# Experts' rows turned by block transpositions on VectorE, and layer 1's experts with two pieces at least, in a two-layer diffusion backbone with a mixture of experts

## The reference

```python
def _grouped_moe(t, router_w, router_b, w_gate, w_up, w_down):
    ...
    gates = jnp.sum(jax.nn.one_hot(e_idx, N_EXPERTS, dtype=jnp.float32) * w[..., None], axis=1)
    y = jnp.zeros(t.shape, jnp.float32)
    for e in range(N_EXPERTS):
        he = jax.nn.silu(t @ w_gate[e]) * (t @ w_up[e])
        y = y + gates[:, e:e + 1] * (he @ w_down[e]).astype(jnp.float32)
    return y.astype(t.dtype)
```

## Time and profile before

| | us |
|---|---|
| median of 3 runs | 1245.73 (1242.93 to 1247.1) |
| the profiled execution, its own time | 1249.11 |
| its span | 1247.4 |
| PE busy | 955.2 (77%) |
| DVE busy | 418.5 (34%) |
| ACT busy | 363.0 (29%) |
| POOL busy | 66.2 (5%) |
| moved by DMA | 326.56 MB, mean 262 GB/s |

### The profile page before, as it was taken

How to read it: one execution, slowest core, us unless ns; L and a number is a source line. 1 busy time by engine, 2 the same in 40 slices (tenths; PEclk the granted TensorE clock), 3 DMA queues, 4 the chain that set the end, 5 groups by cost and what they waited for, 6 DMA issues and landing times.

```text
span 1247.4 us, 23521 instructions
## 1 busy us (share of the span) xinstructions
PE 955.2 (77%) x9105; PEld 549.4 (44%) x9106; DVE 418.5 (34%) x1124; ACT 363.0 (29%) x744; POOL 66.2 (5%) x106
## 2 busy tenths in 40 slices
PE   5799989989962887888888836998993755556883
PEld 3244554433442443444444415785573422323542
DVE  1366655663143111111111217568624100100112
ACT  3322355552031122222222215227612111110221
POOL 0000000000002000000000020000001000000001
PEclk9899999998966998999999976999996977887995
DMA  9999398797033298896989957005045799999942
GB/s 327 403 354 320 134 387 315 272 337 270 0 135 143 75 337 298 325 361 248 398 302 398 367 204 272 1 19 202 1 145 201 274 396 395 395 393 396 397 174 105
DMA packets 139502, 326.56 MB, mean 262 GB/s; under 512 B 9456, under 2 KB 18048, under 8 KB 139456
## 3 DMA queue, kind: packets, MB, share of 16 engines
q1 hardware_dynamic: 118064, 294.36, 63.4%
q0 software_dynamic: 7200, 22.81, 5.2%
q10 hardware_dynamic: 14192, 8.76, 2.3%
HBM read 308.99 MB, written 33.69 MB: 275 GB/s over the span
## 4 chain that ended last, share of the span: by engine, by line
PE 40%; DMA 12%; SPq 10%; ACT 8%; issue 7%; DVE 6%; ACTq 5%; POOL 1%; DVEq 1%; POOLq 0%
SPq L280 9%; PE bank L592 7%; PE bank L524 7%; PE bank L572 5%; ACTq L823 4%; DMA h_t<-h_rows 4%; PE bank L424 4%; PE bank L494 3%; DMA y_rows<-work 3%; ACT L817 3%; PE bank L367 3%; PE bank L465 2%; DMA ring<-in_w_up_dram 2%; PE bank L477 2%; PE bank L535 1%
## 5 line engine op out<-in xcount | busy, mean ns | idle before, releaser
L572 PE MATMUL bank<-ring,h_t 128*32 128x256 f32 x4160 | 259.1, 405 | 68.8 <-DMA ring<-in_w_up_dram 58.7
L572 PEld LDWEIGHTS bank<-ring,h_t 128*32 128x32 f32 x4160 | 140.9, 117 | 173.5 <-issue 103.8
L592 PE MATMUL bank<-ring,h_t 128*32 128x256 f32 x2080 | 130.7, 393 | 21.5 <-issue 16.2
L817 ACT ACT_TABLE_LOAD x65 | 83.4, 1283 | 154.8 <-issue 145.1
L424 PE MATMUL bank<-h_t,ring 128*128 128x512 f32 (+1 forms) x320 | 118.1, 524 | 12.3 <-ACT h_t L732 12.3
L1157 DVE TENSOR_TENSOR h_t<-h_t,bank 128x128 f32<-128x128 f32 x65 | 18.7, 288 | 257.3 <-ACT h_t L817 257.3
L1154 DVE COPY h_t<-bank 128x256 f32<-128x256 f32 x65 | 27.6, 425 | 213.1 <-PE bank L572 209.6
L563 PE MATMUL bank<-cst,h_t 128*128 128x128 f32 x134 | 29.8, 304 | 87.5 <-DVE h_t L1147 87.5
L592 PEld LDWEIGHTS bank<-ring,h_t 128*32 128x32 f32 x2080 | 66.5, 112 | 65.9 <-issue 31.6
L424 PEld LDWEIGHTS bank<-h_t,ring 128*128 128x128 f32 x320 | 62.5, 196 | 60.7 <-issue 40.9
L524 PE MATMUL bank<-tokm,ring 128*128 128x512 f32 (+1 forms) x256 | 85.3, 496 | 1.0 <-DVE tokm L1019 1.0
(11 more groups left out here) (148 smaller groups left out, 1028.6 us busy)
## 6 DMA issues: line engine op xcount, KB each, us to landing
ring<-in_w_gate_dram SPq DMA_DIRECT2D x32, 2048.0 KB, 13.6
ring<-in_w_up_dram SPq DMA_DIRECT2D x32, 2048.0 KB, 17.4
ring<-in_w_down_dram SPq DMA_DIRECT2D x32, 2048.0 KB, 16.5
ring<-in_ada_w_dram SPq DMA_DIRECT2D x24, 2048.0 KB, 10.1
ring<-in_w_in_dram SPq DMA_DIRECT2D x8, 1536.0 KB, 17.8
h_t<-h_rows POOLq DMA_DIRECT2D x70, 128.0 KB, 5.2
h_rows<-in_table_dram SPq DMA_DIRECT2D x1, 8704.0 KB, 45.0
y_rows<-in_table_dram SPq DMA_DIRECT2D x1, 8704.0 KB, 64.0
```

Of the source, the lines that this page charges most:

```text
L572: last = mm(bank[1][CHUNK * q:CHUNK * q + CHUNK, 0:256], hc_t[:, k, :], w[q // 2][:, k, 256 * (q % 2):256 * (q % 2) + 256], start=(k == 0) ...
L592: last = mm(bank[4][CHUNK * q:CHUNK * q + CHUNK, 0:256], h, wd[:, k, 256 * q:256 * q + 256], start=(k == 0), stop=(k == KF - 1))
L817: do(act_g, turned_he[:, :, 0:2 * CHUNK], ACT.Silu).then_inc(silu_done[l], 1)
```

## The change

Each piece is turned without PE. POOL's load now puts quarter q of the 32 rows on partitions 32q to 32q+31 (`(q c)` split with q outermost), and ACT's copy L809 writes the token rows in an order in which the transposition of 32x32 blocks by DVE gives `hc_t` at once. Gate and up are computed so that partition group q holds, for each of gate and up, columns 32q to 32q+31 of each of the four blocks of 128 (the moving operand has 8 runs of 32 columns out of two slots); then silu and the product read bank 1 directly (ACT L799, DVE L1168 in the new numbering), and one more transposition of blocks on DVE gives `he_t`. `turn_rows`, `turn_he`, bank 3 and bank 5 of the expert part, and the copies L1140 and L1154 are gone.

The stores of result rows move from ACT (four of 32 KB) to POOL (one of 128 KB), and `yrow` has two halves. POOL's loop is: store of piece g, then load of piece g+4; before, it held loads alone. ACT runs silu of g+1 ahead of the copy of g. `LEAST` is [2, 2], so layer 1 takes `expert_long` too, its 11 experts with one piece get a second piece of padding, and w_down's slot is free a piece later. `h_rows` and `y_rows` grow from 2176 to 2304 rows. At the start POOL stores six small blocks of zeros to raise the two semaphores of the stores.

```diff
-LEAST = [2, 1]
+LEAST = [2, 2]
...
-ROWS = P * -(-CHUNK * (max(MAX_CHUNKS) + 3) // P)
+ROWS = P * -(-CHUNK * (max(MAX_CHUNKS) + 5) // P)
...
-                sp.wait_ge(down_mm[l], done)
+                sp.wait_ge(down_mm[l], done + 1)
                 load_expert(l, e + 3, a, (2,))
...
                 def gate_up(g, a):
-                    w = [ring[:, 3 * a + s, :].rearrange("p (k n) -> p k n", k=KD) for s in range(2)]
+                    w = ring[:, 3 * a:3 * a + 2, :].rearrange("p s (k c m) -> p s k c m", k=KD, c=KF)
                     pe.wait_ge(hc_ready[l], g + 1)
+                    pe.wait_ge(he_ready[l], g + 1)
                     for k in range(KD):
                         for q in range(4):
-                            last = mm(bank[1][CHUNK * q:CHUNK * q + CHUNK, 0:256], hc_t[:, k, :],
-                                      w[q // 2][:, k, 256 * (q % 2):256 * (q % 2) + 256],
+                            o = bank[1][CHUNK * q:CHUNK * q + CHUNK, 0:256]
+                            last = mm(o.rearrange("r (s c i) -> r s c i", s=2, c=KF), hc_t[:, k, :],
+                                      w[:, :, k, :, CHUNK * q:CHUNK * q + CHUNK],
                                       start=(k == 0), stop=(k == KD - 1))
                     last.then_inc(gu_mm[l], 1)
...
                     gate_up(g0, a)
-                    turn_rows(g0 + 1)
                     if prev is not None:
                         down(g0 - 1, prev)
-                    weights_in(a, turns, (2,))
-                    turn_he(g0)
                     with pe.Fori(g0 + 1, g1) as g:
                         gate_up(g, a)
-                        turn_rows(g + 1)
+                        weights_in(a, turns, (2,))
                         down(g - 1, a)
-                        turn_he(g)
...
-                with act.Fori(0, all_chunks(act, l)) as g:
-                    act.wait_ge(he_turned[l], g + 1)
-                    do(act_g, turned_he[:, :, 0:2 * CHUNK], ACT.Silu).then_inc(silu_done[l], 1)
-                    act.wait_ge(down_mm[l], g + 1)
-                    act.wait_ge(rows_stored[l], 64 * g + 64)
-                    do(yrow, bank[4][:, 0:256], ACT.Identity).then_inc(rows_ready[l], 1)
-                    act.wait_ge(rows_ready[l], g + 2)
-                    for q in range(4):
-                        act.dma_start(y_rows[bass.ds(CHUNK * g, CHUNK), 256 * q:256 * q + 256],
-                                      yrow[CHUNK * q:CHUNK * q + CHUNK, :]).then_inc(rows_stored[l], 16)
+                def gated(g):
+                    act.wait_ge(gu_mm[l], g + 1)
+                    do(act_g, bank[1][:, 0:P], ACT.Silu).then_inc(silu_done[l], 1)
+
+                def row_out(g):
+                    act.wait_ge(down_mm[l], g + 2)
+                    act.wait_ge(rows_stored[l][0], (g + 2) // 2 * 16)
+                    act.wait_ge(rows_stored[l][1], (g + 3) // 2 * 16)
+                    nc.scalar.copy(yrow[:, bass.ds(g % 2 * 256, 256)], bank[4][:, 0:256]).then_inc(rows_ready[l], 1)
...
+                    gated(0)
+                    with act.Fori(0, total - 1) as g:
+                        gated(g + 1)
+                        row_out(g)
+                    row_out(total - 1)
...
                 with pool.Fori(0, (total + 1) // 2) as m:
                     for i in range(2):
-                        pool.wait_ge(hc_moved[l], 2 * m + 1 + i)
-                        load_rows(2 * m + 2 + i, i)
+                        pool.wait_ge(rows_ready[l], 2 * m + 2 + i)
+                        pool.dma_start(y_rows[bass.ds(CHUNK * (2 * m + i), CHUNK), :].rearrange("r (q c) -> q r c", q=4),
+                                       yrow[:, 256 * i:256 * i + 256]).then_inc(rows_stored[l][i], 16)
+                        pool.wait_ge(hc_moved[l], 2 * m + 3 + i)
+                        load_rows(2 * m + 4 + i, i)
...
+                def rows_turned(n):
+                    dve.wait_ge(hc_moved[l], n + 1)
+                    v.transpose(hc_t.rearrange("p k r -> p (k r)"), hc).then_inc(hc_ready[l], 1)
...
                     dve.wait_ge(gu_mm[l], g + 1)
-                    v.tensor_copy(he, bank[1][:, 0:256]).then_inc(he_ready[l], 1)
                     rows_turned(g + 1)
                     dve.wait_ge(silu_done[l], g + 1)
-                    v.tensor_tensor(he_t, act_g, turned_he[:, :, 2 * CHUNK:P], ALU.mult).then_inc(het_ready[l], 1)
+                    v.tensor_tensor(he, act_g, bank[1][:, P:2 * P], ALU.mult).then_inc(he_ready[l], 1)
+                    dve.wait_ge(he_ready[l], g + 2)
+                    dve.wait_ge(down_mm[l], g + 1)
+                    v.transpose(he_t.rearrange("p k r -> p (k r)"), he).then_inc(het_ready[l], 1)
                     rows_in(g + 2)
```

More of the change, by code:

```diff
@@ L142, in backbone @@
         h_rows = nc.dram_tensor("h_rows", [ROWS, D], F32, kind="Internal").ap()
-        y_rows = nc.dram_tensor("y_rows", [ROWS, D], F32, kind="Internal").ap()
+        y_rows = nc.dram_tensor("y_rows", [ROWS + CHUNK, D], F32, kind="Internal").ap()
         ident = cst[:, C_ID:C_ID + P]
@@ L174, in backbone @@
         hc_got = hflat[:, 0:512]
-        hc = hflat[:, 1280:1536]
-        hc_t = hflat[:, 512:768].rearrange("p (k r) -> p k r", k=KD)
-        he = hflat[:, 768:1024]
-        act_g = hflat[:, 1024:1152].rearrange("p (j m) -> p j m", j=2)
-        he_t = hflat[:, 1152:1280].rearrange("p (j m) -> p j m", j=2)
+        hc = hflat[:, 512:768]
+        hc_t = hflat[:, 768:1024].rearrange("p (k r) -> p k r", k=KD)
+        act_g = hflat[:, 1024:1152]
+        he = hflat[:, 1152:1280]
+        he_t = hflat[:, 1280:1408].rearrange("p (k r) -> p k r", k=KF)
         pos = work[:, 736:744]
-        yrow = work[:, 0:256]
+        yrow = work[:, 0:512]
         ych = [tokm, hflat.rearrange("p (t n) -> p t n", t=4)]
@@ L210, in backbone @@
         mask_ready, rank_mm, route_ready = sem("mask_ready"), sem("rank_mm"), sem("route_ready")
[L211 removed]
+        rows_zeroed, block_zeroed = sem("rows_zeroed"), sem("block_zeroed")
         hc_in = [[sem(f"hc_in{l}_{i}") for i in range(2)] for l in range(DEPTH)]
[L213 removed]
+        hc_moved, hc_ready = per_layer("hc_moved"), per_layer("hc_ready")
         gu_mm, silu_done, he_ready = per_layer("gu_mm"), per_layer("silu_done"), per_layer("he_ready")
[L215 to L216 removed]
+        het_ready, down_mm, rows_ready = per_layer("het_ready"), per_layer("down_mm"), per_layer("rows_ready")
+        rows_stored = [[sem(f"rows_stored{l}_{i}") for i in range(2)] for l in range(DEPTH)]
         pos_ready, scattered, rows_all = sem("pos_ready"), sem("scattered"), sem("rows_all")
@@ L221, in backbone @@
         dve_step = sem("dve_step")
-        turned_he = bank[3][:, 0:256].rearrange("p (j m) -> p j m", j=2)
         def ada_bank(u):
@@ L589, in down @@
                     for k in range(KF):
-                        h = he_t[:, k % 2, CHUNK * (k // 2):CHUNK * (k // 2) + CHUNK]
                         for q in range(4):
-                            last = mm(bank[4][CHUNK * q:CHUNK * q + CHUNK, 0:256], h,
+                            last = mm(bank[4][CHUNK * q:CHUNK * q + CHUNK, 0:256], he_t[:, k, :],
                                       wd[:, k, 256 * q:256 * q + 256], start=(k == 0), stop=(k == KF - 1))
@@ L630, in experts @@
                 pe.wait_ge(route_ready, l + 1)
-                turn_rows(0)
                 expert(0, 0, 1, None)
@@ L655, in combine @@
                     tile_sums(nt - 1)
+            for l in range(DEPTH):
+                pe.sem_inc(down_mm[l], 1)
             pe.wait_ge(cst_in, 16)
@@ L808, in route @@
                     act.wait_ge(h_turned, 2 * sum(TOK_TILES[:l]) + q + 1)
-                    do(tokm[:, q // 2, 512 * (q % 2):512 * (q % 2) + 512], bank[2 + q % 4][:, :],
+                    rows = tokm[:, q // 2, :].rearrange("p (j k i) -> p k j i", j=4, k=KD)
+                    do(rows[:, 4 * (q % 2):4 * (q % 2) + 4],
+                       bank[2 + q % 4][:, :].rearrange("p (k j i) -> p k j i", k=4, j=4),
                        ACT.Identity).then_inc(tok_ready, 1)
@@ L869, in _ @@
                 norm_shift(2 * l, 512)
+                if l == 0:
+                    for stored in rows_stored:
+                        act.wait_ge(stored[0], 16)
+                        act.wait_ge(stored[1], 32)
                 qkv(l)
@@ L883, in _ @@
         def _(pool):
-            for l in range(DEPTH):
-                pool.sem_inc(rows_stored[l], 64)
+            pool.wait_ge(block_zeroed, 1)
+            for turns in (1, 2):
+                for l in range(DEPTH):
+                    for i in range(turns - 1, 2):
+                        pool.dma_start(y_rows[ROWS:ROWS + CHUNK, :].rearrange("r (q c) -> q r c", q=4),
+                                       ring[:, 8, 0:256]).then_inc(rows_stored[l][i], 16)
+                        pool.wait_ge(rows_stored[l][i], 16 * turns)
             for l in range(DEPTH):
@@ L907, in load_rows @@
```

(8 more changed lines are left out.)

57 lines of the change are left out of this document (26 added, 31 removed).

## The result

| | before | changed |
|---|---|---|
| median, us | 1244.33 (4 runs, 1240.24 to 1247.1) | 1275.13 (4 runs, 1272.29 to 1275.4) |
| ratio, 95% interval | 1 | 1.0245 (1.0211 to 1.0279) |
| span of the profiled execution | 1247.4 | 1273.2 |
| PE / DVE / ACT / POOL busy | 955.2 / 418.5 / 363.0 / 66.2 | 955.6 / 421.8 / 288.8 / 142.9 |

The account below looks back on a forecast made before the run. Bound in layer 0 by a circle of latencies through ACT (7.52 us a piece), in layer 1 by weights at 395 GB/s. -67.5 + 4 - 1.4 = -64.9 us took the 1245.7 us median to 1181 us; range 1164 to 1210.

Parts of the forecast that it names:

- All of it hangs on 395 GB/s: Layer 0's weight stream: 91.8 MB at layer 1's measured 395 GB/s takes 232 us, so the layer ends at 668.
- a longer landing L: Row loads behind a store in POOL's queue: landing taken as 7 us instead of 5.3, bounds 5.3 and 12.
- Layer 0: Layer 0's experts become a stream of weights; last down at 668 instead of 735.5, a gain of 67.5 us.
- 12.9 us: End of layer 0: gate/up, down, gate/up, down, down after expert 15's w_gate and w_up land, 12.9 us.
- Both signs of being wrong: Prediction wrong if layer 0's last down comes after 690 or layer 1's stretch grows by over 8 us.
- Layer 1: Layer 1's experts, 34 pieces with padding, bound by 90.4 MB of weights and rows: end 1217.0 against 1218.4, -1.4 us.
- Behind the layers: Between the layers: layer 1 transfers queued in the gather's way, +4 us, bounds 0 and 8; after layer 1, 0.
- The w_in and w_out of layer 1 that I feared: Between layers: these 8.4 MB queue behind expert 15 until about 681 and delay the gather, +4 us.
- Rival 3: Less bandwidth: row stores to HBM push a full DMA share to 354 GB/s in both layers; 1234 us, chance 0.03.
- Rival 1: Rows come late through POOL's queue, landing about 12 us, 6.3 us a piece in layer 0; 1195 us, chance 0.19.
- the bound of 8.5: Rows through POOL: four pieces need 13.3 + L, which bounds the loop of a piece above L = 8.5.
- one rival on PE: Gate/up reads its 32-column runs slowly; at twice the time a piece takes 9.05 us, 1374 us; chance 0.06.

Follow-up runs that it names:

- experiment 1: Changed kernel with POOL's row loads, stores and zero block walking HBM straight as (row, quarter), so rows come out permuted: 1194.66 us, ratio 0.9598.
- experiment 3: Changed kernel with LEAST = [2, 1], so no padding pieces in layer 1 (23 instead of 34): 1257.52 us, ratio 1.0109.
- experiment 4: Kernel before with the row load alone changed to (quarter, row), stores and all else as before: 1271.2 us, ratio 1.023.
- experiment 9: Changed kernel with the row stores alone split into four transfers of 32 partitions, loads still in quarters: 1273.52 us, ratio 1.024.
- (11): Kernel of experiment 1 plus, behind each row load, a further 128 KB load in quarters that no compute engine reads: 1299.5 us, ratio 1.0439.
- (8): Changed kernel with the row loads alone split into four transfers of 32 partitions, stores still in quarters: 1234.59 us, ratio 0.9925.

## Why the prediction was wrong

**The step that failed** is "All of it hangs on 395 GB/s, which I take because 160 us of the same kind of work ran at it". It was not the same kind of work. The diff turned `(r q) c` into `q r c` in the loads and put the stores into that pattern. I had costed this at a longer landing L and no more, as though a transfer held nothing but itself. The runs show instead that a load of this pattern slows the weight transfers beside it: 337 GB/s (450 to 600) and 353 (1020 to 1150) for 395, and 395 again in both stretches when only the pattern is made straight. That 4 engines carry it is read from the count of packets. The rule stands in the section of the Trainium skill named above; by it 4 engines were to be expected, and the trace agrees with its count, but neither page nor trace had a price for the weights beside it.

With the measured rate the sum's own working nearly holds. Layer 0: 427.0 + 91.8 MB / 339 GB/s (270.8) + 1 + 7.6 = 706.4; measured 712.6. With 395 GB/s it gives the 668 of the forecast; experiment 1, which holds 395 from 430 to 660, measured 674.3. So the sum is 6 us short in both. Some 3 of them in experiment 1 and 2 in the changed kernel lie behind the last w_up, where the sum has 12.9 us and PE took 16.1 and 15.0: after 4.01 and 8.18 us of idling the first gate/up took 6.26 and 5.15 us instead of 3.59, at a granted clock of 0.54 (658 to 664) and 0.66 (698 to 702). The rest no run divides up. Both signs of being wrong that the prediction names came (the last down after 690, layer 1 longer by over 8 us).

The forecast missed the profiled span by 90.7 us (+25.8 against -64.9), term by term:
- **Layer 0**: the last down was to come 67.5 us earlier and came 22.9 earlier (712.6 instead of 668), 44.6 short. Making the pattern straight gives 38.6 back.
- **Layer 1**: -1.4 forecast, +35.2 measured, 36.6 off. 23 of them go with the padding too (experiment 3: 284.5 to 261.4), whose pieces I priced at 0.66 us, that is at 395 GB/s. The straight pattern gives back 32.
- **Behind the layers**: +4 forecast between them and 0 at the end, +10.7 and +2.9 measured, and for another reason. I had left "4.4 us after the last down, as now" for the first gather. POOL's timeline after:
```profile
715.31 0.70 POOL L924 DMA_DIRECT2D y_rows<-work  x1 [2.70 <-ACT work L805]
718.88 0.68 POOL L912 DMA_DIRECT2D h_t<-h_rows  x1 [2.86 <-issue]
728.34 1.02 POOL L937 DMA_INDIRECT tokm<-y_rows,posidx  x1 [8.79 <-POOLq L933]
```
  The last load, of padding rows that nobody needs, is now issued behind the last store, and the gather stands 8.79 us for it; it starts 15.7 us after the last down (4.5 before). In experiment 1 that was 8.7 us. The w_in and w_out of layer 1 that I feared cost nothing visible: from the first gather to the first matmul of the combination it takes 9.1 us (737.43) and took 8.9 (748.85).

**Rival 3** had the right quantity with a wrong cause, at a chance of 0.03: 354 GB/s and 1234 us. Stores of rows as such don't do it (experiment 1 stores as many at 395). **Rival 1**, late rows, is real but small on PE (25.5 us); the L of 8.9 lies just above the bound of 8.5 that I had worked out.

**Right:** a piece of 5.18 us (5.45 forecast), the transposition at 445 ns (0.4), no price on runs of 32 columns, the gone table loads, the stage turning into a stream of weights. With the pattern straight (experiment 1, whose rows are permuted) the time is 1194.7 us, 14 above the forecast of 1181 and inside its range.

The chance of 0.05 for slower came from one rival on PE. The sum had a single bandwidth in it, and the range left it fixed (354 stood outside). A range that let that one number go down to the lowest full-share rate of the trace would have reached 1234, and still not 1275.

## What to carry to other kernels

Read the slowest dimension of each transfer's access pattern, not its bytes: row transfers with 4 there cost 11 to 15% of the bandwidth (from 395 GB/s to 353 and 337), most of it the weights', although the rows were a tenth of the bytes. Look at the loads first; the stores in that pattern cost little here. When a change re-orders a transfer's dimensions, test the pattern alone in the old kernel first (experiment 4: +2.3% from one line), and where the layout forces a small outer dimension, split the transfer along it (1220.5 for 1275.1 us here). And before a rate measured at a full DMA share is carried over to a changed kernel, ask whether the transfers in that stretch keep their form; a full share at fewer GB/s is the sign that they don't.

## What the hardware showed that I had not expected

- A transfer through POOL's queue with slowest dimension K leaves (16 - K) x 32/K packets of 16 bytes beside its 32 of 4,096: 224, 96, 32 and 0 for K = 2, 4, 8 and 16. The weights' own packets last longer beside it: those of 4,096 B 187.8 ns on average in the changed kernel, 170.8 before, those of 2,048 B 95.8 and 89.7. So the busy share stays full while the rate falls.
- One load of 128 KB in this pattern for each piece brought the rate between 450 and 600 to 336 GB/s, whether an engine needed its data (experiment 9) or not (11); the same pattern in the stores alone left 367 (8).
- The issue of such a load on POOL is longer with a small K: 797, 684, 590 and 525 ns for K = 2, 4, 8 and 16 (549 ns for the straight load).
- With K = 16, pieces of 1 KB taken out of order still cost a little against the straight block: 275.0 and 268.1 us for layer 0, 380 and 395 GB/s.
- DVE's float32 transposition of 32x32 blocks takes 445 ns at 128x256 and 312 ns at 128x128, against 295 ns for a copy of 128x256: by these rows some 180 ns and 1.04 ns per column.
